# A hybrid decoder trunk on one core: router weights as the stationary operand, and the residual's copy in layer two moved to ScalarE

## The reference

```python
h = rms_norm(x, norm_mix)
proj = h @ w_in                      # 4120 columns: delta-rule, retention and mLSTM heads, gates
x = x + mix @ w_out                  # mix: the three kinds of heads, normalised and gated
h = rms_norm(x, norm_ffn)
group_prob = softmax(h @ router_group)             # 4 groups, the best one is taken
expert_logits = h @ router_expert + router_bias    # 8 experts in it, the best two are taken
x = x + sum_e combine[:, e] * (silu(h @ gate[e]) * (h @ up[e])) @ down[e]    # 32 experts
```

## Time and profile before

| | us |
|---|---|
| median of 3 runs | 818.68 (817.82 to 820.04) |
| the profiled execution | 816.45 |
| its span, first to last instruction | 814.7 |
| TensorE busy (PE) | 778.4 (96%) |
| its weight loads (PEld) | 550.1 (68%) |
| VectorE busy | 314.2 (39%) |
| ScalarE busy | 204.3 (25%) |
| data moved | 254.02 MB, 312 GB/s over the span |

### The profile page before, as it was taken

One profiled execution on the slowest core, in us unless ns is written; L12 is line 12 of the kernel. 1 busy time (PEld: TensorE's weight loads), 2 busy tenths in 40 slices (PEclk: granted clock), 3 DMA queues, 4 the chain that ended last, 5 costly groups with the idle time before them and its releaser, 6 DMA issues.

```text
span 814.7 us, 16557 instructions
## 1 busy us (share of the span) xinstructions
PE 778.4 (96%) x6516; PEld 550.1 (68%) x6516; DVE 314.2 (39%) x751; ACT 204.3 (25%) x432; POOL 3.3 (0%) x11
## 2 busy tenths in 40 slices
PE   8999999999999998899999999999999999999976
PEld 7876888878855554465588768888787555554523
DVE  4757243762612111111277563446635111111102
ACT  2443541531410000000214545326212000001003
POOL 1000000000000000000000000000000000000000
PEclk9999999999999999899999999999999999999989
DMA  9952264594999999999996332665949999999995
GB/s 348 418 182 84 99 226 160 158 367 156 379 422 420 419 421 420 421 422 420 418 415 237 130 104 66 221 194 187 366 191 399 422 422 419 422 420 420 420 422 238
DMA packets 41641, 254.02 MB, mean 312 GB/s; under 512 B 4833, under 2 KB 9825, under 8 KB 12769
## 3 DMA queue, kind: packets, MB, share of 16 engines
q1 hardware_dynamic: 40992, 252.22, 77.8%
q10 hardware_dynamic: 576, 0.81, 0.3%
HBM read 250.52 MB, written 1.44 MB: 309 GB/s over the span
## 4 chain that ended last, share of the span: by engine, by line
PE 64%; DMA 14%; DVE 14%; issue 3%; ACT 3%; DVEq 1%; SPq 0%; ACTq 0%; POOLq 0%
DMA ring<-e_down 14%; PE ps L1082 12%; PE ps L623 9%; PE ps L1051 6%; PE ps L960 6%; PE ps L1103 6%; DVE xn L1467 3%; PE ps L1111 3%; PE ps L1115 3%; PE ps L795 3%; PE ps L852 2%; PE ps L821 2%; DVE space L1590 2%; PE ps L652 2%; PE ps L885 1%
## 5 line engine op out<-in xcount | busy, mean ns | idle before, releaser
L623 PE MATMUL ps<-hT,ring 128*128 128x256 f32 x800 | 183.4, 382 | 0.0
L623 PEld LDWEIGHTS ps<-hT,ring 128*128 128x128 f32 x800 | 148.5, 190 | 22.9 <-issue 3.5
L1051 PEld LDWEIGHTS ps<-hT,xn 128*128 128x128 f32 x640 | 73.0, 192 | 9.5 <-issue 7.4
L1051 PE MATMUL ps<-hT,xn 128*128 128x128 f32 x640 | 76.8, 278 | 1.9 <-DVE hT L1816 1.9
L1082 PE MATMUL ps<-space,hT 128*32 128x256 f32 x992 | 64.6, 404 | 9.4 <-DMA space<-e_up 5.7
L1103 PE MATMUL ps<-ring,space 128*32 128x512 f32 x456 | 55.2, 598 | 9.0 <-ACT space L1408 7.6
L960 PE MATMUL ps<-xn,ring 128*128 128x256 f32 x256 | 57.8, 381 | 0.0
L1082 PEld LDWEIGHTS ps<-space,hT 128*32 128x32 f32 x992 | 30.8, 114 | 39.0 <-DMA space<-e_up 11.5
L1816 DVE TENSOR_TENSOR hT<-shapes,sel 128x128 f32<-128x128 f32 x40 | 9.9, 288 | 112.2 <-PE ps L1089 111.9
L960 PEld LDWEIGHTS ps<-xn,ring 128*128 128x128 f32 x256 | 48.1, 190 | 7.2 <-issue 0.7
L1885 DVE COPY hT<-ps 128x512 f32<-128x512 f32 x18 | 12.4, 691 | 90.3 <-PE ps L1103 90.3
(11 more groups left out here) (295 smaller groups left out, 916.8 us busy)
## 6 DMA issues: line engine op xcount, KB each, us to landing
ring<-e_down SPq DMA_DIRECT2D x50, 1024.0 KB, 26.7
ring<-e_up SPq DMA_DIRECT2D x36, 1024.0 KB, 15.4
ring<-w_mix SPq DMA_DIRECT2D x33, 1024.0 KB, 9.5
space<-e_up SPq DMA_DIRECT2D x26, 1024.0 KB, 26.2
space<-e_gate SPq DMA_DIRECT2D x24, 1024.0 KB, 19.5
more_buf<-e_gate SPq DMA_DIRECT2D x14, 1024.0 KB, 10.8
ring<-e_gate SPq DMA_DIRECT2D x8, 1024.0 KB, 8.1
ring<-w_mix SPq DMA_DIRECT2D x14, 512.0 KB, 16.1
```

What stands on the lines that cost most here:

```text
L623: mm = pe.matmul(bank, slot_w(i)[:, k, ct * P:(ct + 1) * P], hT3[:, k, :], start=(k == 0), stop=(k == KD - 1))
L1051: mm = pe.matmul(ps[:, 4 + 3 * half_, kk * P:(kk + 1) * P], xn3[:, j, k * P:(k + 1) * P], Psel[:, j, :], start=(j == 0), stop=(j == TT - 1))
```

## The change

Three things. The router logits are computed with the router weights (128x40) stationary and `xT` (256 tokens) moving, into the bank `logitsT`, 40 rows of 256 tokens; ScalarE copies them to `logT`; and two identity products turn them into the banks that VectorE reads as before. The four turns of the residual are spread between: one before the identity products, one between them and `nsum`, two after it. And in layer two the four copies of the residual from PSUM to `xT` are made by ScalarE, right after its squares; TensorE waits for them before it writes bank 0 again, and VectorE before it adds the projection.

```diff
-    late += [(("logits", 0), 4), (("logits", 1), 7), ("nsum", 6), ("rank", 5)] + [(("xt", i), i) for i in range(4)]
+    late += [("logitsT", 5), (("logits", 0), 4), (("logits", 1), 7), ("nsum", 6), ("rank", 5)] + [(("xt", i), i) for i in range(4)]
...
+        logT = kq[0:NLOG, 1024:1280]
...
                 gbank = begin("gates")
+                if l:
+                    pe.wait_ge(x_kept, 4)
...
                 pe.wait_ge(rwg_ready, upto(l, rwg_ready, 1))
+                bank = begin("logitsT")
+                for k in range(KD):
+                    if k % 2 == 0:
+                        pe.wait_ge(x_mixed, upto(l, x_mixed, k // 2 + 1))
+                    mm = pe.matmul(bank[0:NLOG, 0:T], rw[:, k, :], xT[:, k, :], start=(k == 0), stop=(k == KD - 1))
+                done(mm, "logitsT")
+
+                def turn_x(j, half_):
+
+                    bank = begin(("xt", 2 * j + half_))
+                    for kk in range(4):
+                        mm = pe.matmul(bank[:, kk * P:(kk + 1) * P], xT[:, half_ * 4 + kk, j * P:(j + 1) * P], c("ident"),
+                                       start=(kk == 0), stop=(kk == 3), skip_group_check=True)
+                    done(mm, ("xt", 2 * j + half_))
+
+                turn_x(0, 0)
+                pe.wait_ge(logits_turned, upto(l, logits_turned, 1))
                 for j in range(TT):
                     bank = begin(("logits", j))
-                    for k in range(KD):
-                        if j == 0 and k % 2 == 0:
-                            pe.wait_ge(x_mixed, upto(l, x_mixed, k // 2 + 1))
-                        mm = pe.matmul(bank[:, 0:NLOG], xT[:, k, j * P:(j + 1) * P], rw[:, k, :],
-                                       start=(k == 0), stop=(k == KD - 1))
-                    done(mm, ("logits", j))
+                    done(pe.matmul(bank[:, 0:NLOG], logT[:, j * P:(j + 1) * P], c("ident")[0:NLOG, 0:NLOG], start=True, stop=True),
+                         ("logits", j))
+                turn_x(0, 1)
                 bank = begin("nsum")
...
-                for j in range(TT):
-                    for half_ in range(2):
-                        bank = begin(("xt", 2 * j + half_))
-                        for kk in range(4):
-                            mm = pe.matmul(bank[:, kk * P:(kk + 1) * P], xT[:, half_ * 4 + kk, j * P:(j + 1) * P], c("ident"),
-                                           start=(kk == 0), stop=(kk == 3), skip_group_check=True)
-                        done(mm, ("xt", 2 * j + half_))
+                turn_x(1, 0)
+                turn_x(1, 1)
                 bank = begin("rank")
...
                         act.activation(sq_in[:, 2 * i:2 * i + 2, :], ps[:, i, :].rearrange("p (k t) -> p k t", t=T), ACT.Square).then_inc(squared, 1)
+                    for i in range(4):
+                        act.activation(xT[:, 2 * i:2 * i + 2, :], ps[:, i, :].rearrange("p (k t) -> p k t", t=T), ACT.Copy).then_inc(x_kept, 1)
...
                     act.activation(hT3[:, 2 * n:2 * n + 2, :], xT[:, 2 * n:2 * n + 2, :], ACT.Square).then_inc(x_squared, 1)
+                bank = get("logitsT")
+                act.activation(logT, bank[0:NLOG, 0:T], ACT.Copy).then_inc(logits_turned, 1)
+                act.wait_ge(logits_turned, upto(l, logits_turned, 1))
+                act.sem_inc(free[bank_of["logitsT"][0]], 1)
                 bank = get("nsum")
...
                     TTn(hT3[:, k, :], hU[:, k, :], rstd_row[:, :], ALU.mult).then_inc(hT_ready, 1)
-                if l:
-                    for i in range(4):
-                        link(dve.tensor_copy(xT[:, 2 * i:2 * i + 2, :], ps[:, i, :].rearrange("p (k t) -> p k t", t=T)))
...
+                if l:
+                    dve.wait_ge(x_kept, 4)
                 for n in range(D // COLS):
                     bank = get(("wo", n))
```

More of the change, by code:

```diff
@@ L398, in trunk @@
         x_mixed = sem("x_mixed", 4)
+        x_kept = sem("x_kept")
+        logits_turned = sem("logits_turned", 1)
         x_squared = sem("x_squared", 4)
```

## The result

| | before | after |
|---|---|---|
| median, runs side by side (12 each) | 818.75 us | 823.51 us |
| lowest to highest | 817.40 to 822.89 | 819.87 to 824.84 |
| ratio of after to before | | 1.0039, 95% interval 1.0023 to 1.0056 |
| the profiled execution | 816.45 | 821.77 |
| its span | 814.7 | 820.0 |

The kernel became slower by 0.39%, 3.2 us, with 1.9 and 4.6 as the ends of the interval. On the 818.68 us of the first table that is 821.9, inside the predicted 817.2 to 823.4 and 1.5 above the predicted 820.4. The plain median of after, 823.51, lies a hair above that range. The ratio isn't the quotient of the two medians, which is 1.0058, or 4.8 us; the text goes by the ratio and its interval throughout. The forecast was "within 0.3%": the ratio lies just outside, its interval on both sides.

What follows compares the result with a forecast made beforehand. The bound was taken to be the weight stream with its holes. Terms 0.85 + 1.4 - 1.5 + 1.0 = +1.75 us took the profiled 816.45 to 818.2; the median's 2.2 on top gave 820.4 us, range 817.2 to 823.4.

Steps and rivals of the forecast that it cites:

- Start of layer two: Layer two's start: VectorE loses four copies (2.85 us) to an idle ScalarE; -1.5 us, bounds 0 and -2.85.
- layer one as the pattern of a start without copies: Start to the 16 records: layer one, without the copies, takes 73.34 us, layer two 74.86; hence -1.5.
- No gain at the start: Rival at layer two's start: TensorE bounds it or ScalarE's copies delay rstd; +3.25, 821.9 us; chance 0.08.
- Larger holes: Weight stream around both routers: later slots enlarge its holes, +0.85 us in layer one and +1.4 in layer two.
- TensorE's own speed in the rounds costs nothing: Expert rounds: they end waiting on a weight load, so TensorE's speed there adds no time.
- a DMA share under 0.9 in the rounds: Expert rounds: a DMA share below 0.9 would show the prediction wrong.
- The stream hides the router: Rival in the weight stream: holes don't grow, only the start's -1.5 is left, 817.2 us; chance 0.20.
- Nsum: Router: nsum starts 5.75 us after the router's first record instead of 3.6, 2.1 later.
- The clock: Quiet stretch around rank: one fall of TensorE's clock counted in two layers, +1.0 us, bounds 0 and 3.3.
- the price of one fall: Gather and first expert product: a clock fall costs 0 to 1.63 us, partly spent idle, so 1.0.
- The logits' product: Router: 16 records of 256 columns replace 32 of 40; the product itself gains only 0.2 us.
- Two falls of the clock: Rival: the quiet stretch lowers TensorE's clock in both layers, 1.4 us each; +3.5, 822.2 us; chance 0.27.

Runs made afterwards that it cites:

- experiment 1: Kernel before, with only layer two's four residual copies moved from VectorE to ScalarE, and the waits for them; 818.21 us, ratio 0.9975.
- experiment 4: Changed kernel plus three unused 128x256 products in TensorE's idle time ahead of rank; 819.46 us, ratio 1.0003 to the kernel before.
- Experiment 2: Changed kernel with VectorE's copies in layer two put back, so only the router differs from the kernel before; 825.09 us, ratio 1.0057.
- experiment 6: Changed kernel with the router product spread over two groups of array columns; 819.85 us, ratio 1.0008 to the kernel before.
- Experiment 7: Changed kernel with the router product on two column groups and nsum directly behind the identity products; 817.55 us, ratio 0.9976 to the kernel before.
- experiment 8: Experiment 7 plus two unused 128x256 products in TensorE's idle time ahead of rank; 817.52 us, ratio 0.9976 to the kernel before.
- experiment 5: Kernel before with only nsum moved behind the first two turns of the residual; 824.63 us, ratio 1.0066.

## Why the prediction came out as it did

By the ratios the change can be written as three measured steps: from before to experiment 1 (the start), from there to experiment 4 (the router with the clock held) and from there to after (the clock). The steps add up to the whole by construction, and each is uncertain by about 1.5 us or more, since they come from ratios of different batches. The layers' lengths in the profiles are a second measure.

- **Start of layer two: forecast -1.5, measured -2.0** (ratio 0.9975), and 1.6 between the two profiles of before and after. The step, layer one as the pattern of a start without copies, held: 73.1 to 73.4 us against 74.7 where the clock is the same, though experiment 1's own profile, with a fall of the clock, shows none of it. The rival *No gain at the start* has fallen: ScalarE's copies lie wholly in its idle time.
- **Larger holes: forecast 0.85 + 1.4 = +2.25, measured +2.3** by the ratios (1.0003 - 0.9975 = 0.28%). The windows of experiment 4 give 1.0 more lost in layer one and 1.5 in layer two, so the holes were sized rightly. But its two layers are 405.07 - 401.30 = 3.8 longer than before: both end on TensorE. "TensorE's own speed in the rounds costs nothing" did not hold there. Of the signs named as wrong, one shows at its edge, a DMA share under 0.9 in the rounds: the digit 8 behind layer one's router, which comes from these holes. The rival *The stream hides the router* has fallen.
- **Nsum: forecast 2.1 later, measured 2.5** (6.12 for 3.6). The sum of the products was counted by their weight loads, 0.114 a record, and left out 0.1 to 0.2 at each change of operands: the turn started 3.58 after the router's first record, not 3.47, the identity logits 1.08 behind that, not 0.91, and the second turn 0.57 behind those, not 0.46. Rank came 1.3 and 2.5 later, where 0.9 and 2.1 stood. Y went out 14.39 and 14.29 after the first issue, for 13.9. X in layer one was not later, as forecast (16.25 after the first issue, before 16.33). N0 was forecast at 19.7 in both layers and came at 20.04 in layer two, and at 22.78 in layer one, behind the slow gather.
- **The clock: forecast +1.0, measured +2.9** by the ratios (1.0039 - 1.0003), 1.1 in the lengths of the profiled layers. This is the term that was mis-sized. Its cause was right, and the profile has the one fall in two layers that the text counted, under layer one's gather. The step that failed is the price of one fall: it was taken as at most the 1.63 by which the turns of the kernel before had grown, and partly idle. The fall lasted through the whole gather, 6.46 us for 3.84, and N0 stood right behind it: 5.2 - 2.5 = 2.7 us of the stream, of which 204.30 - 202.49 = 1.8 show in the length of that layer. Experiment 2 shows falls in both gathers; how many there are in an execution varies.
- **The logits' product: forecast no gain worth more than 0.2, measured 3.62 us for 3.65 of weight loads.** The dense product did keep the clock up under the turns (1.00 in 210 to 214 of after). The Trainium skill (TensorEngine Tiling (Array Packing), When to Use Tiling) has the swap go with tiling by columns; experiment 6 agrees for the product, 1.93 for 3.62. Experiment 7 shows what that is worth to this kernel: nsum starts no sooner than before, as it waits for VectorE. What the prediction gave no price is the fall that the dense product avoids: in layer two of experiment 1 it came under the 40-column products, put rank at 13.58 instead of 10.83 and made the layer 1.3 us longer than layer one.

How the loss divides between holes and clock isn't firm: 2.3 and 2.9 by the ratios, 3.8 and 1.1 by the profiled layers. Together they are 5.2 or 4.9, where the prediction had 3.25, and with the start's -1.5 that gives +3.7 or +3.4 against the measured 3.2. That the total of 1.75 fell within the stated range is no proof of its terms. The rival *Two falls of the clock* ended at +3.5, right in the size. The profiled execution has one long fall; it is one of the faster five, with a mean granted clock of 0.991, and the seven slower ones have 0.979 to 0.985. So two or more falls in the usual execution are likely, but not shown.

Experiments 1, 7 and 8 beat the kernel before by the same 0.25%, with 0.05% to 0.11% as the least that their intervals allow. In experiment 1 that is the start of layer two, the only thing changed but the clamp. That it is the same in the other two was not separated: the profile of experiment 7 has a fall in the mixer that hides the gain. Experiment 1 does it with the smallest edit.

## What to carry to other kernels

Before a product is made cheaper, ask which result of the stage is waited for last: here it was a sum of squares, and the cheaper, reordered logits pushed exactly that one back. Where a stream of weights waits for slots, follow the slots, not the engines: in experiment 4 N0 was 1.3 and 2.4 us later than before, and the two layers 1.8 and 2.0 us longer. And when an edit leaves TensorE waiting just ahead of dense work, price the work behind the wait at half clock too, or fill the wait.

## What the runs showed of the hardware

- The granted clock fell to half (1.2 GHz) under products that kept TensorE busy all the time, with 0.3 us idle ahead of them, and stayed there through dense ones behind them. A window of experiment 1, with the 40-column logits and the turns behind them:

```profile
610.00:616.00 6.00, 6.00 (x30) 6.00 (x30) 4.19 (x24) 0.53 (x3) 0.00 (x0) 0.50 1.01 422
```

The clock fell so in 3 of the 6 profiled routers with 40-column products (layer one of before, layer two of experiments 1 and 5). With the router weights stationary it held under the product and the turns in all 14.

- In layer one of after the clock fell in or right behind a stretch that has no long idle gap: 2.14 us idle, 0.8 of short products for rank, 1.07 idle. With 1.28 us in place of the 2.14 (experiment 7) it fell at one router of two, and with the first gap filled (experiments 4 and 8) at none of four. Over all ten profiles, with TensorE's weight loads idle for 1.28 us or more before rank, 9 of 12 gathers ran partly or wholly at half clock; with 1.00 us or less, none of 8. The Trainium skill (TensorE: Matmul & The Clock Gate, Why this matters for your kernels) names idle gaps between bursts as what lowers the clock; the runs agree for the filled gap, and the row above shows that it can fall with no gap over 0.3 us.
- The falls were not of one length: 5.05 to 6.44 us of weight loads for a gather of 3.65.
- Two products on different column groups ran beside each other, 16 records in 1.93 us instead of 3.62, each with its own accumulation in the same bank.
